# ScalarE copies the gate columns of the expert layer, VectorE multiplies in place

## The reference

```python
idx = jnp.take_along_axis(cand_i, pos, axis=-1)
gate = jax.nn.softmax(best_s.astype(jnp.float32), axis=-1).astype(xn.dtype)
...
def block(args):
    xb, ib, gb = args
    act = jax.nn.gelu(jnp.einsum('tkd,td->tk', u_tab[ib], xb), approximate=False)
    return jnp.einsum('tk,tkd->td', act * gb, v_tab[ib])
```

## Time and profile before

| | us |
|---|---|
| median of 3 runs | 1575.96 |
| the three runs | 1586.25, 1575.76, 1575.96 |
| span of the profiled execution, first to last instruction | 1581.1 |
| TensorE busy in that span | 1524.7 (96%) |
| VectorE busy | 1326.5 (84%) |
| ScalarE busy | 720.5 (46%) |
| GpSimd busy | 339.2 (21%) |

### The profile page before, as it was taken

One profiled execution on the slowest core, in us unless ns is written; L12 is line 12 of the kernel. 1 busy time (PEld: TensorE's weight loads), 2 busy tenths in 40 slices (PEclk: granted clock), 3 DMA queues, 4 the chain that ended last, 5 costly groups with the idle time before them and its releaser, 6 DMA issues. The chain is left out here.

```text
span 1581.1 us, 24984 instructions
## 1 busy us (share of the span) xinstructions
PE 1524.7 (96%) x9451; PEld 1388.1 (88%) x9451; DVE 1326.5 (84%) x2360; ACT 720.5 (46%) x1442; POOL 339.2 (21%) x301
## 2 busy tenths in 40 slices
PE   7999799999999999999998999999999999999999
PEld 6898688889998999989998999999999888888887
DVE  4638777776799999988974999998989999999996
ACT  4553454141344698788763333333333334333332
POOL 4011620010466100301220222222322211111100
PEclk9999899999999999999999999999999999999999
DMA  5220004031444567878998999999998999999982
GB/s 197 86 81 1 8 29 160 30 111 50 132 165 153 168 196 214 316 241 282 366 366 312 334 360 354 341 352 328 372 339 315 354 407 376 380 363 340 351 290 97
DMA packets 152236, 384.12 MB, mean 243 GB/s; under 512 B 11072, under 2 KB 92096, under 8 KB 135488
## 3 DMA queue, kind: packets, MB, share of 16 engines
q1 hardware_dynamic: 122176, 232.75, 41.9%
q0 software_dynamic: 18432, 134.23, 23.4%
q10 hardware_dynamic: 11520, 15.73, 2.7%
HBM read 337.58 MB, written 45.09 MB: 242 GB/s over the span
## 5 line engine op out<-in xcount | busy, mean ns | idle before, releaser
L1795 POOL DMA_INDIRECT scores<-in_peer_uv,pair_index x86 | 126.2, 1468 | 620.2 <-DVE pair_sum L1819 503.2
L1984 PE MATMUL bank<-x_hi,u_split 128*128 128x384 f32 x640 | 220.3, 344 | 10.6 <-POOL u_split L1919 5.5
L1986 PE MATMUL bank<-x_hi,u_split 128*128 128x384 f32 x640 | 215.8, 337 | 0.0
L1985 PE MATMUL bank<-x_lo,u_split 128*128 128x384 f32 x640 | 215.6, 337 | 0.0
L2273 PE MATMUL bank<-v_hi,act_hi 128*128 128x512 f32 x528 | 206.2, 391 | 1.0 <-DVE v_lo L2336 1.0
L2275 PE MATMUL bank<-v_hi,act_lo 128*128 128x512 f32 x528 | 205.9, 390 | 0.0
L2274 PE MATMUL bank<-v_lo,act_hi 128*128 128x512 f32 x528 | 205.7, 390 | 0.0
L2352 DVE TENSOR_TENSOR act_tile<-gelu_tile,onehots 128x384 f32<-128x384 f32 x128 | 118.2, 923 | 43.8 <-ACT gelu_tile L2321 33.1
L2310 ACT ACTIVATE act_hi<-act_tile 128x384 fp32r<-128x384 f32 x128 | 66.6, 521 | 182.0 <-PE bank L2275 130.9
L1984 PEld LDWEIGHTS bank<-x_hi,u_split 128*128 128x128 f32 x640 | 121.0, 189 | 13.0 <-issue 5.9
L2261 PE MATMUL bank<-x_hi,u_split 128*128 128x384 f32 x384 | 129.1, 336 | 1.4 <-PEq L1929 1.4
(11 more groups left out here) (325 smaller groups left out, 3625.0 us busy)
## 6 DMA issues: line engine op xcount, KB each, us to landing
v_raw<-in_peer_v SPq DMA_DIRECT2D x128, 512.0 KB
u_raw<-in_peer_u SPq DMA_DIRECT2D x64, 512.0 KB, 7.0
u_raw_more<-in_peer_u SPq DMA_DIRECT2D x64, 512.0 KB, 6.7
gates<-gate_stage SPq DMA_DIRECT2D x24, 1024.0 KB, 6.0
onehots<-gates SPq DMA_DIRECT2D x32, 768.0 KB, 8.9
early_gelus<-early_gelu ACTq DMA_DIRECT2D x80, 192.0 KB
gelu_tile<-early_gelus SPq DMA_DIRECT2D x80, 192.0 KB
w_raw<-in_w_in SPq DMA_DIRECT2D x9, 1024.0 KB, 5.2
```

The source lines that it names most:

```text
L1795: pool.indirect_dma_start(self.slot(k), None, self.table, bass.IndirectOffsetOnAxis(ap=self.sidx[:, k:k + 1], axis=0)).then_inc(self.lande ...
L1984: nc.tensor.matmul(banks.bank(g)[:, 0:TD], uh[:, q, w], m.xh[:, k, P:], start=(k == 0), stop=False)
L1985: nc.tensor.matmul(banks.bank(g)[:, 0:TD], uh[:, q, w], m.xl[:, k, P:], start=False, stop=False)
L1986: t = nc.tensor.matmul(banks.bank(g)[:, 0:TD], ul[:, q, w], m.xh[:, k, P:], start=False, stop=(k == KD - 1))
```

## The change

Two contiguous tiles `act_tile0` and `act_tile1` take the place of `act_tile`. A new function `copy_gate(n)` on ScalarE copies the gate column of group n into tile n % 2, and counts a new semaphore. `gate(n)` on VectorE waits for this count, and multiplies the GELU into the tile in place; it no longer reads the strided column, nor waits for `gated`. `copy_gate(n)` waits for `gated` to reach n-1, that is, until VectorE has taken the low half of group n-2 out of the same tile. On ScalarE it is called for group n+1 in iteration n, behind the GELU and ahead of `split_u(n+2)` and `split_v(n-1)`. The transfers of the next gates wait for the copies and not for the products.

```diff
-        af = m.mem.over("act_tile", [P, TD], "early_gelu")
+        af = [m.mem.over("act_tile0", [P, TD], "early_gelu"), m.mem.take("act_tile1", [P, TD], at_end=True)]
...
-                        sp.wait_ge(gate_f, (it - 1) * BODY)
+                        sp.wait_ge(gate_cols, (it - 1) * BODY)
...
-                    nc.scalar.activation(ah[:, n % NA, :], af[:], ACT.Copy).then_inc(gate_hi, 1)
+                    nc.scalar.activation(ah[:, n % NA, :], af[n % 2][:], ACT.Copy).then_inc(gate_hi, 1)
+
+                def copy_gate(n):
+                    it, jj = n // BODY, n % BODY
+                    if jj == 0:
+                        act.wait_ge(g_in[it % 2], 32 * (it // 2 + 1))
+                    if n >= 2:
+                        act.wait_ge(gated, n - 1)
+                    else:
+                        act.wait_ge(nxt.ge_out[n], 16 * (EARLY // 2))
+                    nc.scalar.activation(af[n % 2][:], gt[:, it % 2, :, jj], ACT.Copy).then_inc(gate_cols, 1)
 
                 split_u(1)
+                copy_gate(0)
...
+                    if n + 1 < NK:
+                        copy_gate(n + 1)
                     if n + 2 < NMT:
                         split_u(n + 2)
...
-                    it, jj = n // BODY, n % BODY
-                    if jj == 0:
-                        dve.wait_ge(g_in[it % 2], 32 * (it // 2 + 1))
-                    if n:
-                        dve.wait_ge(gated, n)
-                    else:
-                        for i in range(2):
-                            dve.wait_ge(nxt.ge_out[i], 16 * (EARLY // 2))
-                    nc.vector.tensor_tensor(af[:], ge[n % NG2][:], gt[:, it % 2, :, jj], ALU.mult).then_inc(gate_f, 1)
+                    dve.wait_ge(gate_cols, n + 1)
+                    nc.vector.tensor_tensor(af[n % 2][:], ge[n % NG2][:], af[n % 2][:], ALU.mult).then_inc(gate_f, 1)
...
-                    nc.vector.tensor_tensor(al[:, n % NA, :], af[:], f(ah[:, n % NA, :]), ALU.subtract).then_inc(gated, 1)
+                    nc.vector.tensor_tensor(al[:, n % NA, :], af[n % 2][:], f(ah[:, n % NA, :]), ALU.subtract).then_inc(gated, 1)
```

More of the change, by code:

```diff
@@ L2157, in experts @@
     up_done, gelu_done, gate_f, gate_hi, gated = (sem(n) for n in ("up_done", "gelu_done", "gate_f", "gate_hi", "gated"))
+    gate_cols = sem("gate_cols_copied")
     down_done, rows_out, out_done = (sem(n) for n in ("down_done", "rows_out", "out_stored"))
```

## The result

The changed kernel takes 1657.53 us (median of 4 runs, 1656.82 to 1658.98), the kernel before 1576.91 (1575.76 to 1586.25): the ratio is 1.0505, with a 95% interval of 1.0478 to 1.0531. It is 80.6 us slower. The forecast was 1643 us, +67, with a range of 1600 to 1658.

A forecast was written before the change was run, and what follows sets the result against it. TensorE bound the kernel before; the new ScalarE-VectorE circle would take over. 44 rounds of 8.50 us, two of 7.36 and 79 of 4.80 led to 1648.1 against 1581.1, +67 on 1575.96: 1643 us, range 1600 to 1658.

The forecast's parts named there:

- The bound before: Both expert stages: TensorE bounds at 8.22 and 4.10 us per group, so VectorE's 47 us less work gains nothing by itself.
- The circle: Closed loop of waits: VectorE's low half, ScalarE's copy and high half, VectorE's low half, pair steps; 8.50 and 4.80 us.
- a round of the first stage: Up-and-down stage, one group's loop through copy, both splits and 3.1 pair steps: 8.50 us against TensorE's 8.22.
- two rounds without u: Two loops without the split of u, before group 47's low half: 7.36 us each, 14.7 together.
- a round of the down-only stage: Groups 47 to 126, one group's loop through copy, split of v and one pair step: 4.80 us against TensorE's 4.10.
- group 126's low half to the end: After the last loop: 2.18 us to the low half of v, `down(126)` 4.10, then 7.44 from `down(127)`'s first matmul.
- the price of the copy: ScalarE's strided copy of 128x384: 0.86 us taken, with 0.52 and 1.15 as ends; 0.75 to 0.95 given chance 0.68.
- The contiguous rate: Rival: ScalarE's strided copy costs only 0.52 us, time 1602 us; chance 0.17 for this or little above it.
- TensorE stays the bound: Rival: ScalarE has the high half of v ready in time, so the kernel is not slower, 1575 us; chance 0.06.
- The clock falls: Rival: TensorE's waits of 0.7 us in every 4.8 lower its clock to 1.2 GHz, about 1915 us; chance 0.02.
- The product stays at 923: Rival: VectorE's gate product stays at 923 ns because of its second source, time 1643 us as well; no separate chance.
- What was to be seen: Signs of being right: copy 0.8 to 0.9 us, product 0.55, the named waits, and low-half starts 4.8 and 8.5 us apart.

## Why the prediction was right, and where it was off

**The bound before.** Right: TensorE, with VectorE's 47 us worth nothing (the contiguous product in the kernel before: 1.0017).

**The circle.** Right, link by link. Forecast for the down-only stage: copy at 0.60, high half of v at 1.36, its low half at 2.45, next round at 4.80. In the round above: 0.59, 1.47, 2.55, and 5.09 for a round with the small product, which costs 0.2 more; over 79 rounds the mean is 4.91. The starts of the low half for groups 1, 45, 47 and 126, as in the earlier trace rows:

```profile
859.48 0.55 DVE L2363 TENSOR_TENSOR act_lo<-act_tile,act_hi 128x384 fp32r<-128x384 f32 x1
...
1237.55 0.56 DVE L2363 TENSOR_TENSOR act_lo<-act_tile,act_hi 128x384 fp32r<-128x384 f32 x1
...
1252.34 0.55 DVE L2363 TENSOR_TENSOR act_lo<-act_tile,act_hi 128x384 fp32r<-128x384 f32 x1
...
1640.27 0.55 DVE L2363 TENSOR_TENSOR act_lo<-act_tile,act_hi 128x384 fp32r<-128x384 f32 x1
```

They give all terms of the sum:

| term | forecast | measured |
|---|---|---|
| first up matmul to group 1's low half | 866.8 - 850.8 = 16.0 | 859.48 - 843.1 = 16.4 |
| a round of the first stage (44) | 8.50 | (1237.55 - 859.48)/44 = 8.59 |
| two rounds without u | 14.7 | 14.8 |
| a round of the down-only stage (79) | 4.795 | (1640.27 - 1252.34)/79 = 4.91 |
| group 126's low half to the end | 13.8 | 14.8 |

The total is 67.0 forecast, 81.7 measured. The rounds hold 44 x 0.09 + 79 x 0.115 = 13 of the 14.7 us between them, the other terms the rest. The last term was 1.0 short for a reason of its own. The sum let `down(126)` start as soon as its low half of v was done, 2.18 us after the low half of the activation. But TensorE was still in `down(125)`, and got to `down(126)` only 3.24 us after it:

```profile
1643.51 0.40 PE L2274 MATMUL bank<-v_hi,act_hi 128*128 128x512 f32 x1
```

**The step that was off** is the price of the copy: "I take 0.86", where it is 0.972. Both ways of working it out were too low. VectorE's surcharge of 0.368 us for the same stride was taken over, or one more of ScalarE's 0.822 ns for each element; the surcharge is 0.45 us, 1.17 ns for each of 384 elements (0.972 against 0.524 for the contiguous copy in the same place). Put into the same sum, 0.97 adds 125 x 0.11 = 14 us and gives 1657. That the range held the result was luck. 1657.53 is 0.5 us under its top of 1658, and one of the four runs (1658.98) lies beyond; a copy over 0.95 us had been given a chance of 0.07, and the range was said to leave out most such copies.

**The rivals.** *The contiguous rate* would have been 1602 us; with the copy made contiguous it was 1604.7, so the time of that case was right to 3 us, and only its premise, the copy at 0.52 us, was wrong. *TensorE stays the bound*: it doesn't as the change stands, but does, to 5 us, with the copy's place or its wait changed (1576.6 and 1581.0). *The clock falls*: no, 1.00 with TensorE waiting in every group. *The product stays at 923*: no, 0.552 us.

**What was to be seen.** The waits for the high half of v were forecast at over 100 us and are 123.6, those of u's at 1.3 each and are 1.5; TensorE's at some 50 and are 54.5. The copy was to be at 0.8 to 0.9 and is not.

## What to carry to other kernels

Before work is moved to an engine with idle time, write down what stands behind it in that engine's queue and what it waits for, and add up the closed loop: here an instruction of 0.97 us, waiting for VectorE's newest result with VectorE's next input queued behind it, set the pace at 4.91 us per group where the bound was 4.10. The same wait cost nothing measurable with the copy at the end of the loop body, and 5 us with one buffer more. And VectorE at 96% busy was not the bound beside a full TensorE: taking 47 us off it gave nothing.

## What was not expected of the hardware

In this kernel ScalarE paid for single fp32 elements that are 16 or 32 bytes apart, but hardly for a step of 8 bytes: 384 elements took 0.511, 0.537, 0.890 and 0.969 us at steps of 4, 8, 16 and 32 bytes. The page "SBUF — State Buffer" of the Trainium skill (Specifications) says that a 16-byte line must be hit at least twice for full bandwidth, which is where the edge lies in these four numbers; the rise from 16 to 32 bytes is not in that rule. The surcharge of the same column was 0.37 us on VectorE and 0.45 on ScalarE, so that the move made the strided read dearer, not only later.
